# Two transformer blocks on one core: two bias tables stored another way, attention's softmax one head ahead, a norm in pairs of chunks

## The chip, the core and the metric

The kernel runs on 1 core of one Trainium2 chip. The metric is device time in microseconds (us) of one execution, lower is better. Engines are named as in the profile: PE is TensorE's matmuls, PEld its weight loads, DVE is VectorE, ACT ScalarE, POOL GpSimd, SP SyncE; ACTq and SPq are the DMA instructions that ACT and SP issue.

## The reference

Two blocks in a row over 256 tokens of width 2048, batch 1, all in float32. The parts that the change touches:

```python
# first block
mod = silu(c) @ w_ada + b_ada              # 2048 x 12288, split in six rows of 2048
shift_m, scale_m, gate_m, shift_f, scale_f, gate_f = split(mod, 6)
h = rms_norm(x, norm_mix_g) * (1 + scale_m) + shift_m
q, k, v, xs, z, bmat, cmat, dt = split(h @ w_in)
attn = rms_norm(moba_attention(q, k, v, rel_bias), attn_norm_g)  # 8 heads of 128; at 256
       # tokens plain causal: softmax(q k / sqrt(128) + rel_bias[rel_bucket(i - j)]) v
ssm = ssd_mixer(xs, z, bmat, cmat, dt, ...)    # conv of 4 taps, silu, state space, norm
x = x + gate_m * (concatenate([attn, ssm]) @ w_out)
h = rms_norm(x, norm_ffn_g) * (1 + scale_f) + shift_f
x = x + gate_f * conv_ffn(h, w_up, conv_w, conv_b, w_down)       # 2 x 5632 wide
x = rms_norm(x, final_norm_g)
# second block: neighbourhood attention on a 4 x 64 grid, its bias read from
# na_rpb (8 heads, 15, 31); latent attention; attention to a memory of 256 rows; swiglu
```

## The kernel before

**The weights** come as one stream of 442 tiles of 128 x 2048 float32 (1 MB), in the order of `STREAM`: xk, xv (keys and values of the memory, needed in the second block), xs, dt, bz, qkv, wb, wa, up, down, then the second block's. A tile is two halves; half h of the program is 24 matmuls of 256 columns (`half_T`) or 12 of 512 (`half_N`), because each product is made of three: high part by high part, low by high, high by low. So for each half ACT writes `w_hi` (`hi`, L474), POOL writes `w_lo` as the difference (L454), and PE multiplies (L1091 to L1095, L1105 to L1109). There are four slots for w_hi and w_lo and a ring of four raw tiles; SP issues tile t when POOL is done with the halves of tile t-4. The halves that matter here: xk from 0, xv from 32, xs from `hx` = 64, dt 80, bz from `hb` = 82, qkv from `hq` = 106, wb from 154, wa from `ha` = 170, up from `hu` = 186.

**The modulation rows.** silu(c) @ w_ada isn't made on PE: DVE adds up 192 rows of 128 x 1024 (0.5 MB each, `ada_row`, L1646, L1649), 32 for each sixth of `mod`. SP issues them between the tiles of the stream into a ring of four slots for the first 80 and of two slots behind that (`ADA_EARLY`). When they are used is set by the table `ROW_POINTS`, by straight lines between its points: `rows_by(h)` is the number of rows due at half h. SP issues by it (L401 to L411), and DVE calls `rows_to(h)` at many places between its other work. When 32 rows are in, ACT copies the sum (`slice_out`, L590, for the first three slices), PE sums over the partitions (`ada_sum`, 16 products with a column of ones, L1167), and DVE adds the bias (`ada_mod`). `ada_sum(4)` stands at PE ahead of half ha+12 and waits for all of the first 160 rows.

**The two tables.** Both attentions read their bias from DRAM with skewed access patterns. For the first, DVE leaves 8 rows of 512 in SBUF (`tab_row`), and ACT stores them 128 times each, one DMA of 1024 pieces of 2 KB into `rel_rows` (L612). For the neighbourhood one, 56 rows of 31 values are loaded into zeroed rows of 127 and stored 64 times each, 3584 pieces of 508 bytes into `rpb_rows` (L614). ACT issues both behind its tenth high part. ACT's DMAs run on queue q10, SP's on q1.

**Attention of the first block.** For each head u: PE `scores(u)`, DVE `front(u)` (bias and maximum, L1756, L1760), ACT `exp_head(u)` (L530), DVE `back(u)` (1/sum times the row, L1771, L1775), PE `turn(u)` (four transposes, L1345), ACT `copies(u)`, PE `values(u)` (L1358), ACT `moba_operand(u)` (L549, L551), DVE `moba_low(u)` (L1781). PE places two or three halves of qkv and wb in each turn of the loop (`beside`). DVE's turn u is `front(u+1)`, `back(u)`, `moba_low(u-1)`, `rows_to`.

**Output projection and feed-forward norm.** wa has four groups of four halves. After each, `wa_out(q)` scales the sum by the gate and the attention's row into SBUF (L2059), adds it to `res` (L2064) and signals; ACT squares that quarter of `res` (L494), DVE adds the squares up (L1701). ACT issues w_hi for the next halves behind its wait for that residual (L777 to L780). Ahead of `wa_out(q)` DVE brings its rows to ha+4q+4. After `wa_out(3)`: sum of squares over the partitions on PE (L1176), `means` and `root` on DVE (three Newton steps, L1676 to L1695), `token_scaled` (L1726), scale and shift on ACT (L787), `a_hi` (L505), `a_lo` (L1711), each in quarters of 4 chunks; then PE starts `up`.

## Time and profile before

| | |
|---|---|
| median of 3 runs | 3019.35 us (3014.46 to 3024.26) |
| profiled execution, its own time | 3018.35 us |
| its span | 3016.6 us |
| PE busy | 2789.4 us (92%) |
| PEld / POOL busy | 2711.5 us (90%) / 2197.0 us (73%) |
| DVE / ACT busy | 1072.8 us (36%) / 1210.7 us (40%) |
| mean granted TensorE clock | 0.955 of full speed |
| DMA | 589.75 MB, mean 196 GB/s |

The span is the stretch between the first and the last instruction in the trace; the execution's own time is 1.75 us longer. A busy PE is not PE at its peak: its matmuls overlap, so the time to look for is idle time ahead of a matmul, with what released it, and stretches where the granted clock is under 1.

### The profile page before, as it was taken

Reading aid. Unit: us, or ns where it says so; the run is one execution under the profiler, and the core shown is the slowest. Engines: PE = TensorE matmul, PEld = TensorE weight load, DVE = VectorE, ACT = ScalarE, POOL = GpSimd, SP = SyncE. Lnnn points to the kernel's source line nnn. Section 1 sums busy time; section 2 is a strip of 40 time slices with the busy share of each in tenths; the row PEclk is TensorE's granted clock in tenths of the full one; section 3 lists DMA queues with packets and bytes.
Section 4 is the critical chain, followed back from the end, with each engine's and each line's share of the span. In section 5 each row is a group of like instructions: output and inputs, shape, how many; then the busy total and the mean of one; then the engine's idle time right before and its main releaser. Section 6 shows DMA issues by size and latency. Waiting matters only on the chain.

```text
span 3016.6 us, 52183 instructions
## 1 busy us (share of the span) xinstructions
PE 2789.4 (92%) x21360; PEld 2711.5 (90%) x21360; DVE 1072.8 (36%) x1251; ACT 1210.7 (40%) x1439; POOL 2197.0 (73%) x889
## 2 busy tenths in 40 slices
PE   4799998977599999999999988999999999999997
PEld 3788998867599999999999977899999999999996
DVE  4554446646444544432235324461030000002233
ACT  3335343332253433334455344453353333334442
POOL 3577665545478889878888864586788888887894
PEclk7899899988799999999999999999999999999998
DMA  9897656555346666544545543363445555554552
GB/s 318 307 368 273 225 223 256 211 195 188 140 168 223 229 227 232 202 154 180 181 167 182 189 158 115 112 224 140 154 169 182 184 183 184 184 181 159 184 184 86
DMA packets 111618, 589.75 MB, mean 196 GB/s; under 512 B 23276, under 2 KB 25324, under 8 KB 54796
## 3 DMA queue, kind: packets, MB, share of 16 engines
q1 hardware_dynamic: 92592, 570.47, 52.0%
q10 hardware_dynamic: 18908, 17.58, 2.1%
q8 instruction: 90, 1.47, 0.2%
q14 instruction: 28, 0.23, 0.0%
HBM read 577.79 MB, written 10.21 MB: 195 GB/s over the span
## 4 chain that ended last, share of the span: by engine, by line
POOL 36%; issue 32%; PE 29%; DVE 1%; POOLq 1%; ACT 0%; DVEq 0%; ACTq 0%
POOL w_lo L454 36%; PE ps L1091 10%; PE ps L1095 10%; PE ps L1093 10%; POOLq L453 0%; PE ps L1176 0%; DVE res L2393 0%; POOLq L457 0%; ACT w_hi L474 0%; PE ps L1167 0%; DVE stage_v L1701 0%; DVE res L2064 0%; DVE ps L1685 0%; DVE ps L1682 0%; DVE rstd L1687 0%
## 5 line engine op out<-in xcount | busy, mean ns | idle before, releaser
L454 POOL TENSOR_TENSOR w_lo<-raw,w_hi 128x1024 fp32r<-128x1024 f32 x884 | 2196.6, 2499 | 785.8 <-ACT w_hi L474 783.0
L1091 PE MATMUL ps<-a_hi,w_hi 128*128 128x256 f32 x6512 | 1874.7, 288 | 117.2 <-POOL w_lo L454 43.5
L1093 PE MATMUL ps<-a_lo,w_hi 128*128 128x256 f32 x6512 | 1860.5, 286 | 0.0
L1095 PE MATMUL ps<-a_hi,w_lo 128*128 128x256 f32 x6512 | 1859.7, 286 | 0.0
L474 ACT CAST w_hi<-raw 128x1024 fp32r<-128x1024 f32 x884 | 918.3, 1047 | 1296.4 <-PE ps L1095 1135.4
L1091 PEld LDWEIGHTS ps<-a_hi,w_hi 128*128 128x128 f32 x6512 | 1270.2, 195 | 127.5 <-issue 52.7
L1093 PEld LDWEIGHTS ps<-a_lo,w_hi 128*128 128x128 f32 x6512 | 1269.7, 195 | 0.8
L1095 PEld LDWEIGHTS ps<-a_hi,w_lo 128*128 128x128 f32 x6512 | 1268.2, 195 | 0.0
L1808 DVE TENSOR_TENSOR a_lo<-arena,a_hi 128x1024 fp32r<-128x1024 f32 x44 | 107.6, 2448 | 348.4 <-ACT a_hi L816 348.4
L2356 DVE TENSOR_TENSOR work<-ps,rstd 128x512 f32<-128x512 f32 x22 | 15.2, 692 | 430.4 <-PE ps L1095 430.4
L1649 DVE SCALAR_TENSOR_TENSOR ps<-arena,small,ps 128x1024 f32<-128x1024 f32 x90 | 113.7, 1286 | 127.6 <-DMA arena<-ada 127.2
L1822 DVE TENSOR_SCALAR work<-ps,vec 128x256 f32<-128x256 f32 x100 | 47.5, 539 | 255.2 <-PE ps L1095 255.2
L1649 DVE SCALAR_TENSOR_TENSOR arena<-arena,small 128x1024 f32<-128x1024 f32 x60 | 111.3, 1865 | 74.0 <-DMA arena<-ada 73.6
L1105 PE MATMUL ps<-w_hi,a_hi 128*128 128x512 f32 x264 | 110.8, 420 | 5.0 <-POOL w_lo L454 5.0
L1107 PE MATMUL ps<-w_hi,a_lo 128*128 128x512 f32 x264 | 107.5, 407 | 0.0
L1109 PE MATMUL ps<-w_lo,a_hi 128*128 128x512 f32 x264 | 106.8, 404 | 0.0
L2119 DVE SCALAR_TENSOR_TENSOR arena<-arena,small 128x1024 f32<-128x1024 f32 x32 | 83.5, 2632 | 45.3 <-DMA arena<-ada 44.7
L1827 DVE SCALAR_TENSOR_TENSOR work<-ps,vec,work 128x255 f32<-128x255 f32 (+2 forms) x212 | 87.6, 476 | 5.5 <-DVE work L1822 2.4
L1105 PEld LDWEIGHTS ps<-w_hi,a_hi 128*128 128x128 f32 x264 | 52.6, 199 | 16.7 <-POOL w_lo L454 5.5
L1732 DVE TENSOR_TENSOR arena<-ps,rstd 128x1024 f32<-128x1024 f32 (+1 forms) x19 | 23.0, 1208 | 122.4 <-PE ps L1095 122.3
L1711 DVE TENSOR_TENSOR a_lo<-work,a_hi 128x1024 fp32r<-128x1024 f32 x24 | 46.2, 1926 | 50.8 <-ACT a_hi L505 50.8
L1109 PEld LDWEIGHTS ps<-w_lo,a_hi 128*128 128x128 f32 x264 | 52.4, 199 | 11.7
(181 smaller groups left out, 1266.5 us busy)
## 6 DMA issues: line engine op xcount, KB each, us to landing
raw<-stream SPq DMA_DIRECT2D x442, 1024.0 KB, 4.8
arena<-ada SPq DMA_DIRECT2D x192, 512.0 KB, 5.7
arena<-memT SPq DMA_DIRECT2D x4, 512.0 KB, 11.1
rel_rows<-arena ACTq DMA_DIRECT2D x1, 2048.0 KB
res<-xT SPq DMA_DIRECT2D x1, 2048.0 KB, 23.4
k_spill<-arena ACTq DMA_DIRECT2D x4, 512.0 KB, 8.7
v_spill<-arena ACTq DMA_DIRECT2D x4, 512.0 KB, 7.2
work<-rel_rows ACTq DMA_DIRECT2D x16, 128.0 KB, 2.2
```

The source lines that it names most:

```text
L454: pool.tensor_tensor(w_lo[:, h % SLOTS], raw_half(h), w_hi[:, h % SLOTS].bitcast(F32), ALU.subtract).then_inc(lo_ready, 1)
L474: act.copy(w_hi[:, base % 4], raw[:, tile_slot, (base % 2) * HALF:(base % 2 + 1) * HALF]).then_inc(hi_ready, 1)
L1091: pe.matmul(o, w_hi[:, h % SLOTS, w], a_hi[:, c0 + k, :], start=first and k == 0 and f % 2 == 0, stop=False, skip_group_check=True)
L1093: pe.matmul(o, w_hi[:, h % SLOTS, w], a_lo[:, c0 + k, :], start=False, stop=False, skip_group_check=True)
L1095: mm = pe.matmul(o, w_lo[:, h % SLOTS, w], a_hi[:, c0 + k, :], start=False, stop=last and k == 1, skip_group_check=True)
L1105: pe.matmul(out2[:, t, 0:width], a_hi[:, c0 + k, a], w_hi[:, h % SLOTS, w], start=first and k == 0, stop=False, skip_group_check=True)
L1107: pe.matmul(out2[:, t, 0:width], a_lo[:, c0 + k, a], w_hi[:, h % SLOTS, w], start=False, stop=False, skip_group_check=True)
L1109: mm = pe.matmul(out2[:, t, 0:width], a_hi[:, c0 + k, a], w_lo[:, h % SLOTS, w], start=False, stop=last and k == 1, skip_group_check=True)
L1649: ins = dve.scalar_tensor_tensor(out=a, in0=ada_slot(n % ring), scalar=ck, in1=a, op0=ALU.mult, op1=ALU.add)
L1808: dve.tensor_tensor(a_lo[:, a:a + 4, :], hidden[:, 4 * quad:4 * quad + 4, :], a_hi[:, a:a + 4, :].bitcast(F32), ALU.subtract).then_inc(hl_ ...
L1827: ins = dve.scalar_tensor_tensor(out=dst[:, c, shift:S], in0=src[:, c, 0:S - shift], scalar=w(c, taps - 1 - shift), in1=dst[:, c, shift:S] ...
L2119: dve.scalar_tensor_tensor(out=a, in0=ada_slot(s % 2), scalar=small[:, bass.ds(i * 2 + (16 + s // 2), 1)], in1=a, op0=ALU.mult, op1=ALU.ad ...
```

## The change

1. The neighbourhood table comes as an input in the layout in which it is read (56 x 64 x 127), so `rpb_rows`, its memset, its load and its store go.
2. `tab_row` moves to `stage_v`. Its store is cut into 8 DMAs, one head each (128 pieces of 2 KB from one partition), each behind two high parts of the halves 68 to 84.
3. xT is loaded in quarters behind tiles 5 to 8, not whole behind tile 6.
4. `ROW_POINTS` changes: 96 rows are due at half 97, not 104; between 148 and 182 the pace is 18 rows in 18 halves, then 14 in 16.
5. `slice_out(2)` moves up, ahead of the last four high parts of bz.
6. DVE's turn of the attention loop becomes `front(u+1)`, `back(u+1)`, rows, `moba_low(u-1)`.
7. `wa_out` works in PSUM; the rows stand behind it, and the last quarter is done in two halves.
8. The feed-forward norm: PE adds the last quarter's squares up itself, and scale, shift and split go in eight pairs of chunks, PE taking one pair per half.

```diff
-ROW_POINTS = [(-1, 8), (56, 64), (66, 64), (90, 84), (104, 96), (108, 96), (138, 128), (146, 128), (178, 160),
+ROW_POINTS = [(-1, 8), (56, 64), (66, 64), (97, 96), (108, 96), (138, 128), (148, 128), (166, 146), (182, 160),
               (186, 160)]
@@ sync
-                if t == 6:
-                    sp.dma_start(res[:, :, :], xT).then_inc(s_res, 16)
+                if 5 <= t < 9:
+                    q = t - 5
+                    sp.dma_start(res[:, 4 * q:4 * q + 4, :], xT[:, 4 * q:4 * q + 4, :]).then_inc(s_res[q], 16)
@@ scalar
-                if h == 6:
-                    act.wait_ge(rel_row, 1)
-                    act.dma_start(rel_dram, tab_row.unsqueeze(1).broadcast_to([8, P, REL])).then_inc(scr_stored, 16)
-                    act.wait_ge(rpb_in, 16)
-                    act.dma_start(rpb_dram, tab_rpb[:, 0:NA_W].unsqueeze(1).broadcast_to([56, GRID, NA_W]))\
-                       .then_inc(scr_stored, 16)
...
-            his(hx + 4, 8)
+            def rel_rows(h):
+                act.dma_start(rel_dram[h:h + 1], tab_row[h:h + 1].unsqueeze(1).broadcast_to([1, P, REL]))\
+                   .then_inc(scr_stored, 16)
+            for j in range(4):
+                his(hx + 4 + 2 * j, 2)
+                rel_rows(j)
...
-            his(hx + 13, 8)
+            for j in range(4):
+                his(hx + 13 + 2 * j, 2)
+                rel_rows(4 + j)
...
-                    his(hb + 19, 8)
-            slice_out(2)
+                    his(hb + 19, 4)
+                    slice_out(2)
+                    his(hb + 23, 4)
...
-            for q in range(4):
-                his(ha + 3 + 4 * q, 4 if q < 3 else 5)
+            his(ha + 3, 1)
+            for q in range(3):
+                his(ha + 4 + 4 * q, 4)
                 residual_ready("wa")(q)
                 square2(K0["ffn"] + q, res_quad(q))
+            his(ha + 16, 4)
@@ tensor
+            for n in range(8):
+                pe.wait_ge(fl_ready, n + 1)
+                half_of("T", "up", n)
+            groups("T", "up", 1, 22)
@@ vector
             front(0)
+            back(0)
             for u in range(8):
                 if u < 7:
                     front(u + 1)
-                back(u)
+                    back(u + 1)
...
+                rows_to(moba_until(2 * u))
...
-                rows_to(moba_until(2 * u + 1))
...
-            def wa_out(q):
+            def wa_out(q, a, b):
...
             for q in range(3):
-                rows_to(ha + 4 * q + 4)
-                wa_out(q)
+                wa_out(q, 0, 4).then_inc(evac[G % 2], 1)
                 if q:
                     add_up(K0["ffn"] + q - 1, early(q - 1))
+                rows_to(ha + 4 * q + 8)
...
+            def ffn_scaled(p):
+                for j in range(2):
+                    c = 2 * p + j
+                    ins = dve.scalar_tensor_tensor(out=ffn_pair(p)[:, j, :], in0=res[:, c, :], scalar=mod[:, 3, c:c + 1],
+                                                   in1=row_a, op0=ALU.mult, op1=ALU.mult)
+                ins.then_inc(fs_ready, 1)
```

In the order in which ACT issues its instructions, the place behind the last `v_spill` (the start of xs) read, before:

```order
L582 DMA v_spill<-arena 128x1024
L474 CAST w_hi<-raw 128x1024 x9
L663 ACTIVATE arena<-work 128x1024
L474 CAST w_hi<-raw 128x1024 x8
L663 ACTIVATE arena<-work 128x1024
```

and now (L482 is `hi`, L660 the store of one head, L670 the silu of a convolution):

```order
L588 DMA v_spill<-arena 128x1024
L482 CAST w_hi<-raw 128x1024 x2
L660 DMA rel_rows<-stage_v 128x1x512
...
L482 CAST w_hi<-raw 128x1024 x2
L660 DMA rel_rows<-stage_v 128x1x512
L482 CAST w_hi<-raw 128x1024
L670 ACTIVATE arena<-work 128x1024
```

Eight stores stand where none stood, four on each side of the first silu. On DVE, one turn of the attention loop (u = 5) read, before:

```order
L1756 SCALAR_TENSOR_TENSOR work<-ps,work 128x512
L1760 TENSOR_REDUCE small<-work 128x2
L1771 RECIPROCAL small<-small 128x2
L1775 TENSOR_SCALAR work<-work,small 128x256 x2
L1781 SCALAR_TENSOR_TENSOR a_lo<-ps,vec,a_hi 128x256
L1798 SCALAR_TENSOR_TENSOR res<-ps,mod,res 128x256 x4
L1649 SCALAR_TENSOR_TENSOR arena<-arena,small 128x1024 x3
```

and now (L1786 to L1811 are the lines L1756 to L1781 of before, L1679 a modulation row, L1828 the residual):

```order
L1786 SCALAR_TENSOR_TENSOR work<-ps,work 128x512
L1790 TENSOR_REDUCE small<-work 128x2
L1801 RECIPROCAL small<-small 128x2
L1805 TENSOR_SCALAR work<-work,small 128x256 x2
L1679 SCALAR_TENSOR_TENSOR arena<-arena,small 128x1024 x3
L1811 SCALAR_TENSOR_TENSOR a_lo<-ps,vec,a_hi 128x256
L1828 SCALAR_TENSOR_TENSOR res<-ps,mod,res 128x256 x4
```

The reciprocal now belongs to the head of the L1786 above it, and the rows stand ahead of the wait for the values. On DVE around the projection wa the rows (L1649, now L1679) and the residuals (L2059 and L2064, now L2091 and L2095) stood, before, as

```order
L1649 SCALAR_TENSOR_TENSOR arena<-arena,small 128x1024 x8
L2059 SCALAR_TENSOR_TENSOR work<-ps,mod,rstd 128x256 x4
L2064 TENSOR_TENSOR res<-res,work 128x1024
L1649 SCALAR_TENSOR_TENSOR arena<-arena,small 128x1024 x4
L2059 SCALAR_TENSOR_TENSOR work<-ps,mod,rstd 128x256 x4
```

and now

```order
L1679 SCALAR_TENSOR_TENSOR arena<-arena,small 128x1024 x5
L2091 SCALAR_TENSOR_TENSOR ps<-ps,mod,rstd 128x256 x4
L2095 TENSOR_TENSOR res<-ps,res 128x1024
L1679 SCALAR_TENSOR_TENSOR arena<-arena,small 128x1024 x7
L2091 SCALAR_TENSOR_TENSOR ps<-ps,mod,rstd 128x256 x4
L2095 TENSOR_TENSOR res<-ps,res 128x1024
L1731 TENSOR_REDUCE arena<-work 128x256
L1679 SCALAR_TENSOR_TENSOR arena<-arena,small 128x1024 x4
```

Five rows stand ahead of the first residual in place of eight, seven ahead of the second in place of four, and four ahead of the third in place of none.

## Rows read from the trace of the kernel before

**Rows 1.** The page: busy time, and the granted clock in 40 slices.

```profile
PE 2789.4 (92%) x21360; PEld 2711.5 (90%) x21360; DVE 1072.8 (36%) x1251; ACT 1210.7 (40%) x1439; POOL 2197.0 (73%) x889
PEclk7899899988799999999999999999999999999998
```

**Rows 2.** Timeline of PE, start: start us, us, instruction, idle before it, releaser.

```profile
80.48 0.55 PE L1091 MATMUL ps<-a_hi,w_hi 128*128 128x256 f32 x1 [33.44 <-issue]
112.36 0.58 PE L1091 MATMUL ps<-a_hi,w_hi 128*128 128x256 f32 x1 [12.53 <-POOL w_lo L454]
```

**Rows 3.** Timeline of ACT, the same stretch.

```profile
40.55 19.65 ACTq L614 DMA_DIRECT2D rpb_rows<-arena  x1
88.43 20.31 ACTq L582 DMA_DIRECT2D k_spill<-arena  x1
108.84 3.89 ACT L474 CAST w_hi<-raw 128x1024 fp32r<-128x1024 f32 x4 [19.38 <-issue]
```

**Rows 4.** Timeline of DVE, the same stretch.

```profile
73.60 1.29 DVE L1649 SCALAR_TENSOR_TENSOR ps<-arena,small,ps 128x1024 f32<-128x1024 f32 x1 [11.93 <-DMA arena<-ada]
79.90 0.42 DVE L1687 SCALAR_TENSOR_TENSOR rstd<-ps,rstd 128x256 f32<-128x256 f32 x1
```

**Rows 5.** DMA queues in 44 to 46 us, then in 47 to 54 us.

```profile
q10 hardware_dynamic: 103, 0.21, 33.5%
...
q10 hardware_dynamic: 174, 0.36, 45.8%
q1 hardware_dynamic: 90, 0.79, 37.3%
```

**Rows 6.** Windows: busy us by engine (PE, PEld, DVE, ACT, POOL), clock, DMA share, GB/s.

```profile
200.00:240.00 40.00, 40.00 (x178) 33.11 (x177) 17.95 (x14) 17.70 (x19) 35.28 (x16) 1.00 1.02 416
278.00:345.00 67.00, 66.37 (x480) 66.17 (x479) 31.62 (x50) 21.34 (x21) 47.17 (x21) 0.85 0.68 249
606.00:714.00 108.00, 77.88 (x447) 71.02 (x446) 43.95 (x64) 35.55 (x65) 48.39 (x20) 0.86 0.53 189
714.00:793.00 79.00, 54.68 (x398) 53.79 (x396) 47.86 (x50) 19.44 (x22) 39.96 (x17) 0.81 0.49 182
```

**Rows 7.** Timeline of PE and ACT at the third slice's sum.

```profile
422.29 6.99 PE L1167 MATMUL ps<-ones,arena 128*128 128x1 f32 x32 [6.52 <-ACT arena L590]
...
417.33 1.01 ACT L590 COPY arena<-ps 128x1024 f32<-128x1024 f32 x1 [6.25 <-DVE ps L1649]
```

**Rows 8.** Waits in 606 to 714 us: who for whom, total us, times, longest.

```profile
PE ps L1345 <- DVE work L1775: 30.1, 6, 7.2
ACT work L530 <- DVE small L1760: 37.8, 6, 9.4
...
DVE arena L1649 <- DMA arena<-ada: 8.4, 4, 2.6
```

**Rows 9.** Timeline of DVE, one bias of the attention loop, then projection wa.

```profile
685.80 0.69 DVE L1756 SCALAR_TENSOR_TENSOR work<-ps,work 128x512 f32<-128x512 f32 x1
...
759.47 1.28 DVE L1649 SCALAR_TENSOR_TENSOR arena<-arena,small 128x1024 f32<-128x1024 f32 x1 [2.43 <-DMA arena<-ada]
762.36 1.22 DVE L2064 TENSOR_TENSOR res<-res,work 128x1024 f32<-128x1024 f32 x1
```

**Rows 10.** Timeline of PE, projection wa: first stall, sum of the fifth slice.

```profile
768.09 0.58 PE L1091 MATMUL ps<-a_hi,w_hi 128*128 128x256 f32 x1 [14.12 <-POOL w_lo L454]
792.46 4.83 PE L1167 MATMUL ps<-ones,arena 128*128 128x1 f32 x32
```

**Rows 11.** Timeline of DVE, ACT and PE, feed-forward norm.

```profile
810.84 1.66 DVE L2059 SCALAR_TENSOR_TENSOR work<-ps,mod,rstd 128x256 f32<-128x256 f32 x4 [10.51 <-PE ps L1095]
827.88 2.36 DVE L1726 TENSOR_TENSOR work<-res,rstd 128x1024 f32<-128x1024 f32 x2
...
829.14 2.07 ACT L787 ACTIVATE work<-work,mod 128x256 f32<-128x256 f32 x4 [12.61 <-DVE work L1726]
...
833.69 0.55 PE L1091 MATMUL ps<-a_hi,w_hi 128*128 128x256 f32 x1 [11.42 <-DVE a_lo L1711]
```

More of the change, by code:

```diff
@@ L165, in rows_by, with block_program @@
             return n0 + (n1 - n0) * (h - a) // (b - a)
[L168 to L169 removed]
+def block_program(nc, stream, ada, xT, memT, vecs, consts, onehot, relb, rpb_dram, out, rel_dram,
+                  k_dram, v_dram):
     ctx = ExitStack()
@@ L269, in x_out, with ffn_pair @@
             return ps[:, 6:8, :].rearrange("p b (c t) -> p (b c) t", t=S)
+        def ffn_pair(p):
+            return work[:, 2048 + p % 4 * 512:2560 + p % 4 * 512].rearrange("p (c t) -> p c t", t=S)
         def early(k):
@@ L281, in stage @@
             return arena[:, 4096 + g % 2 * 1024:5120 + g % 2 * 1024]
-        s_const, s_vec, s_res = sem("s_const"), sem("s_vec"), sem("s_res")
+        s_const, s_vec = sem("s_const"), sem("s_vec")
+        s_res = [sem(f"s_res{q}") for q in range(4)]
         s_mem = [sem(f"s_mem{q}") for q in range(4)]
@@ L1388, in _ @@
             pe.wait_ge(row_ready, 2)
-            row_sums("ffn", (ps[:, 4, 0:S], early4))
-            groups("T", "up", 0, 22, al=al_before("ffn"))
+            pe.wait_ge(r_ready, NORM["ffn"])
+            for k in range(3):
+                pe.matmul(ps[:, 4, 0:S], ones[:, :], early(k), start=k == 0, stop=False, skip_group_check=True)
+            for p in range(2):
+                if p:
+                    pe.wait_ge(sq2_ready, K0["ffn"] + 4)
+                else:
+                    pe.wait_ge(last_sq, 1)
+                for j in range(2 * p, 2 * p + 2):
+                    mm = pe.matmul(ps[:, 4, 0:S], ones[:, :], sq2(K0["ffn"] + 3)[:, j, :], start=False, stop=j == 3,
+                                   skip_group_check=True)
+            mm.then_inc(r_summed, 1)
+            for n in range(8):
+                pe.wait_ge(fl_ready, n + 1)
+                half_of("T", "up", n)
+            groups("T", "up", 1, 22)
             ada_sum(5)
@@ L1841, in conv_ssm @@
                          lambda c: col("cs_b", 4 * j + c), 4, evac[G % 2])
-            dve.memset(tab_rpb, 0.0).then_inc(rpb_zero, 1)
             link(dve.memset(tab_row[:, S:REL], MASKED))
@@ L2051, in _ @@
             residual_part("wb", 3, 2)
[L2053 removed]
+            rows_to(ha)
+            def wa_out(q, a, b):
                 G = G0["wa"] + q
                 dve.wait_ge(half_used, ha + 4 * q + 4)
[L2057 to L2061 removed]
+                for j in range(a, b):
+                    o = acc(G)[:, j, :]
+                    ins = dve.scalar_tensor_tensor(out=o, in0=o, scalar=mod[:, 2, 4 * q + j:4 * q + j + 1],
+                                                   in1=row_b, op0=ALU.mult, op1=ALU.mult)
@@ L2070, in _ @@
                 if q:
                     add_up(K0["ffn"] + q - 1, early(q - 1))
-            rows_to(ha + 16)
+                rows_to(ha + 4 * q + 8)
+            add_up(K0["ffn"] + 2, early(2))
+            parts_ready(10)
             ada_mod(4)
-            add_up(K0["ffn"] + 2, early(2))
-            wa_out(3)
-            add_up(K0["ffn"] + 3, early(3))
-            parts_ready(11)
+            G = G0["wa"] + 3
+            wa_out(3, 0, 2).then_inc(last_res, 1)
+            link(wa_out(3, 2, 4))
@@ L2078, in _ @@
+            settle()
+            dve.engine_nop().then_inc(last_res, 1)
+            dve.engine_nop().then_inc(evac[G % 2], 1)
             v = ps[:, 4, 0:S]
             means("ffn", (v, D))
+            dve.engine_nop().then_inc(sq2_done, 1)
             root(v, ps[:, 4, S:2 * S], row_a)
-            token_scaled("ffn", 0, 5)
-            token_scaled("ffn", 1, 6)
-            for q in range(4):
-                low_of_ring("ffn", q, 4 * q)
-                if q < 2:
-                    token_scaled("ffn", q + 2, 7 + q)
+            def ffn_scaled(p):
+                for j in range(2):
+                    c = 2 * p + j
+                    ins = dve.scalar_tensor_tensor(out=ffn_pair(p)[:, j, :], in0=res[:, c, :], scalar=mod[:, 3, c:c + 1],
+                                                   in1=row_a, op0=ALU.mult, op1=ALU.mult)
+                ins.then_inc(fs_ready, 1)
@@ new lines, in ffn_low @@
+            def ffn_low(p):
+                dve.wait_ge(fh_ready, p + 1)
+                for j in range(2):
+                    c = 2 * p + j
+                    ins = dve.scalar_tensor_tensor(out=a_lo[:, c, :], in0=ffn_pair(p)[:, j, :], scalar=mod[:, 4, c:c + 1],
+                                                   in1=a_hi[:, c, :].bitcast(F32), op0=ALU.add, op1=ALU.subtract)
+                ins.then_inc(fl_ready, 1)
+            ffn_scaled(0)
+            ffn_scaled(1)
+            for p in range(8):
+                ffn_low(p)
+                if p < 6:
+                    if p >= 2:
+                        dve.wait_ge(fl_ready, p - 1)
+                    ffn_scaled(p + 2)
@@ L2509 @@
     scratch = [nc.dram_tensor(n, s, F32).ap() for n, s in
-               [("rel_rows", [8, P, REL]), ("rpb_rows", [56, GRID, NA_W]), ("k_spill", [4, P, 1024]),
+               [("rel_rows", [8, P, REL]), ("k_spill", [4, P, 1024]),
                 ("v_spill", [4, P, 1024])]]
```

50 lines of the change are left out of this document (23 added, 27 removed).

## The prediction

> **What bounds the kernel now.** I read the page first: PE is busy 92% of the span and its clock is full except in the first third and a few slices behind it [rows 1]. So the time to win is where PE stands idle, and the slow matmuls behind each such stop; the rest of the span is one half of weights after the other, 2.88 us each. I then went through PE's timeline for idle time over 0.8 us. Its largest stops lie at places that this change touches: the start, the third slice's sum, the attention loop, the projection wa, the feed-forward norm. Each place is read from the timelines of the engines PE waits for. Sums are made against the profiled execution's 3018.35 us, 1.0 under the median of 3019.35; I add that 1.0 at the end.
>
> **1. Start: the tables' stores go, -34.** PE stands 33.4 us until 80.5 and 12.5 us until 112.4 [rows 2]. ACT's issue of the 3584 pieces took 19.65 us, and the next issue on its queue, a `k_spill`, 20.31 us, behind the same backlog; ACT converted nothing meanwhile [rows 3]. The first stop ends with DVE's root, which waited for modulation rows: the fourteenth was used at 73.6 and the root ended at 80.3 [rows 4]. What made the row late is on the queues: in 47 to 54 us q10 held 46% of the DMA engines' time and the stream got 0.79 MB in 7 us, 113 GB/s [rows 5], where 416 is had with q10 quiet [rows 6]. Without the stores, row 13 has ahead of it tile 6, a quarter or two of xT and row 12, some 2.5 MB behind 44 us, at 0.41 MB/us 6 us, with some 2 us of latency by 52 to 54; row 13 and the root take 7 [rows 4], so PE starts at about 60: 20 us won. The second stop goes wholly, 12.5. Each stop is followed by matmuls at 0.5 of the clock; one fewer is worth 2 us. Sum 34. Against it, the DMA has less time for the same rows: 25 MB are due between 43 us and the first slice's end, 62 us of transfer where PE leaves 68. So at worst 14 of the 34 come back; at best 37.
>
> **2. The first table head by head, +42.** The 8 stores now fall in 278 to 345 us. The trace has one such store: 8 partitions at once. In its first 2 us it moved 0.21 MB in 103 pieces at 33.5% of 16 engines' time, so 0.10 us of one engine per piece; then, steady, 0.36 MB in 7 us, 51 GB/s from 8 partitions, and by the same sum 0.29 us per piece [rows 5]. A head is 0.26 MB from one partition, on however many engines. Its ends: 16 engines at 0.10 us per piece, 0.8 us; or one partition giving an eighth of 51 GB/s, 41 us. At first a piece of 2 KB, which lies in one partition, took 0.10 us, 20 GB/s, so the slow end is far off; at 20 GB/s a head takes 13 us, at 51 GB/s 5. I take 9, 72 us in all. Meanwhile the stream gets little, as in 47 to 54 us. The stretch has 32% of its DMA time idle, 21 us [rows 6], and the four halves that stand converted ahead of PE cover 11. Three more modulation rows than before (4 us) fall in it too. 72 + 4 - 21 - 11 = 44; rounded to 42, as the dt products, slow and without weights, lie in it. Between the ends the cost is 0 to 270. ACT's own issues (0.4 us each) hide under its 68% idle time.
>
> The profile shows 8 partitions giving 51 GB/s between them when the store runs steadily [rows 5]. The Trainium skill (SBUF — State Buffer, Door 1: The DMA port swizzle) says that DMA bandwidth depends on how many of the 16 ports the partitions reach, four neighbouring partitions sharing one at about 27 GB/s. By that rule the 8 partitions are two ports, and the trace agrees (51); a single partition is one port, an estimate of 9.7 us per head, and this term would be 48 in place of 42.
>
> **3. Third slice's sum, -9.** PE waits 6.5 us for ACT's copy, which waits for DVE's last rows of the slice, and the sum then runs 7.0 us at the low clock [rows 7], where the later one takes 4.8 [rows 10]. With the 96th row due seven halves sooner and the copy ahead of four high parts, wait and slow clock go: 6.5 + 2.2. Not late: at up to 3.7 us per row, 2.4 of wait and 1.3 of work [rows 9], the nine rows behind bz's first convolution (which ends at 368) end near 400 us, and PE needs them at 415.
>
> **4. Attention loop, -30.** `turn(u)` waits for DVE's L1775 six times, 30.1 us [rows 8]. Cause: DVE does `front(u+1)` and `back(u)` only after two or three rows and the wait for the values of head u-1. Now the probabilities for turn u+1 are ready a whole turn early. New waits: `back(u+1)` follows ACT's `exp_head(u+1)`, 1.4 us, within the same turn, and DVE stands through it. A turn of DVE is then some 1.4 (front, two instructions of 0.7 [rows 9]) + 1.5 + 0.8 (back) + 6 (three rows, two of them landed, one at 2.4 + 1.3 [rows 9]) + 0.5, 10.2 us, against PE's 11.2 (three halves and 2.6 of attention); in the first four turns 2 rows and 2 halves stand against each other likewise. ACT waits 37.8 us for the maximum [rows 8]; that shrinks, so the high parts come sooner. The clock over this stretch is 0.86 [rows 6]; with 30 us of stops gone I take 3 us back from it, and give 3 to small new waits.
>
> **5. Projection wa, -13.** The stretch 714 to 793 us has 54.7 us of PE work in 79 [rows 6]. Its largest stop, 14.1 us [rows 10], is ACT waiting for the first residual, which ended at 763.6 behind eight rows [rows 9]. Now five rows stand there, and the first residual is done some 31 us behind the last head's values at 714 (heads' sum 5, root and two residuals 10, rows 13, residual 3), in time. But the others stand behind it. Once DVE waits for each, the ring of two slots gives a row per 3.7 us [rows 9]; beside less POOL work I take 3.3. Seven rows, two of them landed, are 19 us and put the second residual at 53; the last four are in at 64, and `ada_sum(4)` waits for them. PE, with sixteen halves, would be there at 47, and so waits 17 us; before it was there at 792.5 - 714 = 78 [rows 10]. Gain 15, less 2 for a slow clock behind the new stop.
>
> **6. Feed-forward norm, -9.** From the last half of wa to the first matmul of `up`: 810.8 to 833.7, 22.9 us [rows 11]. Its terms now: half a residual 1.7 (2 of the 4 of 1.66, and an add), then square, second half and its products to 5.2, means and root 5.5 (as 74.8 to 80.3 [rows 4]), one pair scaled 0.9, ACT 1.1 (half of 2.07), low part 0.9: 14. Later pairs come every 2 us and a half takes 2.9, so PE doesn't wait again. The ninth high part ACT can only give at about 25 us, needed at 28: just hidden.
>
> Sum: -34 + 42 - 9 - 30 - 13 - 9 = -53; 3018.35 - 53 + 1.0 = **2966 us**. The memset, load and store of the second table cost nothing more, and the second block is untouched.
>
> **The rivals.**
> - *A head's store is quick* (2 us or less). For: 0.10 us per piece at first [rows 5]; 16 engines share it. Against: the steady rate. Then term 2 is 0 to 5: 2926.
> - *The store of one partition starves the stream: slower.* Place: 278 to 360 us. With a head at h us the cost is 8h - 28; it cancels the 95 us won elsewhere at h = 15. For: 51 GB/s over 8 partitions could be a limit of each partition or a clash of 16 engines on one. Against: one engine alone drew 20 GB/s. At h = 20: 132, so 3018 - 95 + 132 = 3055.
> - *The rows' ring sets the pace from 610 to 790.* If the 32 rows of the fifth slice can't go faster than the 3.7 us of [rows 9] when tiles and DVE's other work come between, `ada_sum(4)` moves by 13 of the 43 us of terms 4 and 5 only: 2996. Against: DVE waited only 8.4 us for rows in the loop [rows 8].
> - *The start stays bound by DMA*: the rows land as late as now since xT and tiles fill the queue; only the second stop goes, 22 us less won: 2988.
>
> **How the numbers follow.** Forecast 0.49 (own range 2945 to 2990), quick store 0.20, starved stream 0.12, ring 0.12, start 0.07. A measurement here tells about 0.3%, 9 us, from no change: faster below 3010, slower above 3028. The range goes from the quick store's value with some 10 us of room, 2916, to 3008, above the ring's and the start's; outside lie the starved stream and a tail of the forecast. Faster 0.86 (all but the starved stream, and a little of the others' tails), slower 0.09, same 0.05.
>
> **What would show it.** Right: no ACTq issue near 20 us; PE starts before 65 us and has no second stop by 90. In 280 to 370 us q10 at 25 to 30 GB/s and PE stops of 40 us in all, with DVE waiting for rows. No L1805 wait at PE ahead of 700 us. A wait of some 15 us at the fifth `ada_sum` for DVE's rows. Norm 14 us. Wrong: a head's 128 pieces taking under 3 us or over 13; stops in the loop of over 10 us in all; the second residual ahead of PE's need.

## The result, and the profile after

| | before | changed |
|---|---|---|
| median, us | 3016.9 (3011.1 to 3024.3, 4 runs) | **2964.7** (2962.4 to 2966.8, 4 runs) |
| profiled span, us | 3016.6 | 2960.6 |

The ratio is 0.9824, with a 95% interval from 0.9808 to 0.9839: 52 us less, where 53 less was predicted. The sum is right, but not all of its terms are: terms 2 and 3 together came out 15 us better than forecast and term 5 came out 13 us worse. That they cancel is luck. The spans differ by 56.0 us.

The page of the changed kernel, engines and granted clock [rows 1]:

```profile
PE 2771.9 (94%) x21366; PEld 2694.1 (91%) x21366; DVE 1106.1 (37%) x1274; ACT 1205.9 (41%) x1436; POOL 2211.4 (75%) x889
PEclk8998799998899999999999999999999999999998
```

PE has nearly the same count of matmuls in both, and 17.5 us less of modelled busy time. That is fewer of them at the low clock; the rest of the 56 us is idle time. To place it I set landmarks of PE side by side: the first matmul of a slice's sum (its weights are `ones`, 32 of them in a row), the last product of the last head, and the first matmul of `up`.

```
landmark                          before    after    gained since the one above
first slice's sum                 153.17   119.79    33.4   (term 1: 34)
fourth slice's sum                587.25   571.65   -17.8   (terms 2 and 3: -33)
last head's last product          714.7    666.9     32.2   (term 4: 30)
fifth slice's sum                 792.46   744.27     0.4   (term 5: 13)
first matmul of up                833.69   778.30     7.2   (term 6: 9)
end of the span                  3016.6   2960.6      0.6
```

Everything arises ahead of `up`. The landmark of the fourth sum is good to some 6 us: in four kernels that have the same instructions up to there (the changed one, and those below with the old loop, the old last rows and the old norm) it starts between 571.7 and 578.0 us. PE's timeline of the changed kernel has, in the order of the program, these stops [rows 2, 10, 11]:

```profile
60.80 0.55 PE L1107 MATMUL ps<-a_hi,w_hi 128*128 128x256 f32 x1 [14.37 <-issue]
...
287.29 0.58 PE L1107 MATMUL ps<-a_hi,w_hi 128*128 128x256 f32 x1 [15.56 <-POOL w_lo L462]
...
672.59 0.58 PE L1107 MATMUL ps<-a_hi,w_hi 128*128 128x256 f32 x1 [5.27 <-DVE res L1828]
...
744.27 6.96 PE L1183 MATMUL ps<-ones,arena 128*128 128x1 f32 x32 [18.49 <-issue]
...
778.30 0.58 PE L1107 MATMUL ps<-a_hi,w_hi 128*128 128x256 f32 x1 [8.40 <-DVE a_lo L2130]
```

The first stop ends at 60.8, where about 60 was expected, and there is no second one until the stores of the table. The last but one is the wait that the new order makes, 18.5 us at the fifth sum. Windows of the changed kernel, to be read against [rows 6]: the table's stores, the attention loop, projection wa, the norm. (Columns as there: busy us of PE, PEld, DVE, ACT and POOL, clock, DMA share, GB/s.)

```profile
245.00:325.00 80.00, 53.48 (x383) 52.98 (x381) 25.69 (x42) 14.26 (x14) 37.22 (x16) 0.75 1.00 175
590.00:667.00 77.00, 71.02 (x453) 65.34 (x451) 61.43 (x60) 38.30 (x73) 56.08 (x20) 0.96 0.66 231
667.00:744.00 77.00, 49.95 (x388) 48.59 (x386) 63.75 (x56) 19.91 (x22) 50.69 (x18) 0.85 0.58 216
744.00:778.00 34.00, 24.04 (x142) 22.66 (x142) 17.31 (x33) 8.08 (x11) 11.93 (x5) 0.75 0.37 140
```

In the first, the DMA engines are busy all the time and move 175 GB/s. PE lacks weights for a third of the stretch, and ACT and POOL, which prepare them, are idle too. In the second, the clock is 0.96 where it was 0.86, and PE is busy 92% of the time. The waits of that stretch (who for whom, total us, times, longest) have no line for the probabilities any more [rows 8]; the new ones are small:

```profile
DVE small L1801 <- ACT work L538: 8.1, 7, 1.2
...
PE ps L1361 <- DVE a_lo L1811: 4.6, 2, 3.0
```

In the third window, DVE is busy 63.8 us of 77, the largest share that it has anywhere in the table.

### The profile page after: what moved, and what is told of

It is laid out like the page before. It is cut to its first block, busy times and chain, and to the rows that moved or that the text cites. A ratio compares the mean times of both kernels' runs of the same rounds, so it can differ in the third digit from the quotient of the medians.

```text
span 2960.6 us, 52233 instructions
## 1 busy us (share of the span) xinstructions
PE 2771.9 (94%) x21366; PEld 2694.1 (91%) x21366; DVE 1106.1 (37%) x1274; ACT 1205.9 (41%) x1436; POOL 2211.4 (75%) x889
## 4 chain that ended last, share of the span: by engine, by line
POOL 37%; issue 31%; PE 30%; DVE 1%; POOLq 1%; ACT 0%; DVEq 0%; ACTq 0%
POOL w_lo L462 37%; PE ps L1107 10%; PE ps L1109 10%; PE ps L1111 10%; POOLq L461 0%; PE ps L1183 0%; POOLq L465 0%; DVE res L2448 0%; PE ps L1192 0%; DVE stage_v L1731 0%; ACT w_hi L482 0%; DVE ps L1715 0%; DVE ps L1712 0%; DVE rstd L1717 0%; DVE ps L2091 0%
## 5 line engine op out<-in xcount | busy, mean ns | idle before, releaser
L482 ACT CAST w_hi<-raw 128x1024 fp32r<-128x1024 f32 x884 | 918.4, 1047 | 1262.1 <-PE ps L1111 1124.3
L1679 DVE SCALAR_TENSOR_TENSOR ps<-arena,small,ps 128x1024 f32<-128x1024 f32 x90 | 114.1, 1286 | 141.2 <-DMA arena<-ada 140.9
L1679 DVE SCALAR_TENSOR_TENSOR arena<-arena,small 128x1024 f32<-128x1024 f32 x60 | 142.8, 2397 | 50.4 <-DMA arena<-ada 50.2
L2174 DVE SCALAR_TENSOR_TENSOR arena<-arena,small 128x1024 f32<-128x1024 f32 x32 | 84.8, 2670 | 44.0 <-DMA arena<-ada 43.5
L1123 PEld LDWEIGHTS ps<-w_hi,a_lo 128*128 128x128 f32 x264 | 52.2, 198 | 10.5
```

The source lines that it names most:

```text
L482: act.copy(w_hi[:, base % 4], raw[:, tile_slot, (base % 2) * HALF:(base % 2 + 1) * HALF]).then_inc(hi_ready, 1)
L1123: pe.matmul(out2[:, t, 0:width], a_lo[:, c0 + k, a], w_hi[:, h % SLOTS, w], start=False, stop=False, skip_group_check=True)
L1679: ins = dve.scalar_tensor_tensor(out=a, in0=ada_slot(n % ring), scalar=ck, in1=a, op0=ALU.mult, op1=ALU.add)
L2174: dve.scalar_tensor_tensor(out=a, in0=ada_slot(s % 2), scalar=small[:, bass.ds(i * 2 + (16 + s // 2), 1)], in1=a, op0=ALU.mult, op1=ALU.ad ...
```

## The experiments

The first question was the table: what do the eight stores cost, and what makes them slow? The landmarks give terms 2 and 3 only together. (Pieces and rows taken one by one, here and below, are from the trace's records; medians are of 2 to 5 runs.)

**Stores taken from all 128 partitions.**

```diff
-tab_row = stage_v[0:8, 0:REL]
+tab_row = stage_v[:, 0:REL]
+tab_wide = arena[0:32, 6656:6784]
...
-pe.matmul(ps[0:8, 1, 0:S], tab_rel, tab_hot[:, 0:S],
+pe.matmul(ps[:, 1, 0:S], tab_wide, tab_hot[:, 0:S],
...
+dve.tensor_copy(tab_wide.rearrange("p (h r) -> p h r", r=16), tab_rel.unsqueeze(2).broadcast_to([32, 8, 16]))
...
-act.dma_start(rel_dram[h:h + 1], tab_row[h:h + 1].unsqueeze(1).broadcast_to([1, P, REL]))
+act.dma_start(rel_dram.rearrange("h (q r) n -> (h q) r n", r=8)[:, h], tab_row)
```

> The changed kernel (2964.7 us), with each row of the first table made sixteen times (128 partitions instead of 8) and each of the eight stores taken from all 128 partitions, 128 pieces of 2 KB as before and at the same places of the program. In the changed kernel a head's store takes 7.1 to 10.4 us and its pieces 0.81 us each in the mean. Theory A, the reading side is what is slow (one partition gives some 28 GB/s): pieces fall to 0.10 to 0.16 us, a store to 1 to 2 us, and nearly all of the 30.6 us that PE loses between the first half of xs and the first of qkv comes back: 2935 to 2943 us. Theory B, many small writes of 2 KB are slow whatever they are read from: 2965 us, a store still 7 to 10 us.

Measured: 2934.8 us, ratio to before 0.9721 (0.9705 to 0.9737).

**Stores from four neighbouring partitions**, from the same widened table:

```diff
-act.dma_start(rel_dram[h:h + 1], tab_row[h:h + 1].unsqueeze(1).broadcast_to([1, P, REL]))
+act.dma_start(rel_dram[h].rearrange("(q r) n -> q r n", r=32),
+              tab_row[16 * h:16 * h + 4].unsqueeze(1).broadcast_to([4, 32, REL]))
```

> The changed kernel (2964.7 us), with head h stored from four neighbouring partitions (16h to 16h+3), 32 pieces of 2 KB from each, at the same places. Theory A1, four neighbouring partitions share one way out: a store takes 8 to 10 us as from one partition, 2965 us. Theory A2, each partition has its own limit of some 28 GB/s: 2.5 us per store, 2938 to 2946 us. Theory B (the writes are slow): 2965 us as well, and only the run with 128 partitions tells it from A1. The Trainium skill (SBUF - State Buffer, Door 1) is on the side of A1: four neighbouring partitions share one port of about 27 GB/s; by it a store of 0.26 MB is an estimate of 9.7 us here too.

Measured: 2951.5 us, ratio 0.9772 (0.9755 to 0.9788), between the two theories.

**No stores.**

```diff
-                rel_rows(j)
...
-                rel_rows(4 + j)
...
-            act.wait_ge(scr_stored, 16 * NH)
...
+            "rel": np.broadcast_to(np.pad(a["rel_bias"][onehot[:, :S].argmax(0)].T[:, None, :], ((0, 0), (0, 0), (0, REL - S)),
+                                          constant_values=MASKED), (8, P, REL))
```

> The changed kernel without the eight stores of the first table: its rows come as an input, gathered when the inputs are laid out. It prices the whole of the stores. If they alone cost the 30.6 us between the first half of xs and the first of qkv: 2932 to 2937 us, with PE's stops near 287, 325 and 369 us gone. Rival: modulation rows and the dt products hold PE there anyway: 2950 to 2960 us.

Measured: 2933.2 us, ratio 0.9718 (0.9701 to 0.9734). So the stores cost 31.5 us, and from 128 partitions, where a store takes 2.2 us in the mean, next to nothing (1.6 us, within the intervals). The DMA queues in 240 to 330 us: the changed kernel, where ACT's queue is q10 (with it 272 pieces of other stores) and SP's is q1:

```profile
q10 hardware_dynamic: 1296, 2.62, 59.3%
q1 hardware_dynamic: 2786, 14.55, 39.2%
```

The same with stores from four partitions:

```profile
q1 hardware_dynamic: 4020, 20.49, 66.4%
q10 hardware_dynamic: 1200, 2.62, 11.2%
```

And from 128:

```profile
q1 hardware_dynamic: 4878, 24.62, 72.2%
q10 hardware_dynamic: 1296, 2.62, 8.1%
```

The windows of the same kernels over the 84 us of the stores, changed kernel first, then four partitions, then 128:

```profile
244.00:328.00 84.00, 56.82 (x397) 56.32 (x398) 28.55 (x48) 17.01 (x17) 39.01 (x18) 0.74 0.99 182
```

```profile
244.00:328.00 84.00, 74.15 (x532) 73.45 (x531) 34.93 (x52) 22.79 (x23) 52.28 (x23) 0.84 0.78 258
```

```profile
244.00:328.00 84.00, 83.36 (x622) 83.16 (x621) 42.66 (x62) 26.71 (x26) 61.17 (x26) 0.88 0.81 311
```

The bytes on q10 are the same in all three. From one partition they hold 59% of the engines' time, from 128 they hold 8%, and q1 moves 24.6 MB in place of 14.6. One 2 KB piece takes 0.81 us in the mean from one partition and 0.09 from 128. The run with four partitions separates two things. Its stores are no quicker: eight of them one behind the other from 245.2 to 323.0 us, 2.1 MB at 27 GB/s, and a head's store in the changed kernel takes 7.1 to 10.4 us from its first piece to its last, 8.6 in the mean, 31 GB/s. So four neighbours give together no more than one gives, and A2 falls. Yet the stream gets 20.5 MB beside these stores, which hold 11% of the engines' time. **With the same bytes in about the same time, the store that holds more of the engines' time costs the others more**: 31.5 us with the long pieces, 18 with the short ones. The 18 us come with the engines' time nearly free of the stores, so the share isn't all of it. The tiles of the stream still land late beside the four partitions (issues in 240 to 330 us, the last number is the median time to landing; changed kernel, four partitions, 128):

```profile
raw<-stream SPq DMA_DIRECT2D x10, 1024.0 KB, 18.8
```

```profile
raw<-stream SPq DMA_DIRECT2D x12, 1024.0 KB, 17.6
```

```profile
raw<-stream SPq DMA_DIRECT2D x14, 1024.0 KB, 6.6
```

What holds them is not shown.

The Trainium skill (SBUF — State Buffer, Door 1: The DMA port swizzle) gives about 27 GB/s to four neighbouring partitions that share a port, and the run with four partitions agrees, 27 GB/s. A second page (DMA: Bandwidth & Descriptors, Why a DMA increments its semaphore by 16 and not by 1) says that the slowest dimension longer than one sets how many engines a DMA is spread over: by it 16 for the 128 rows, four for the 4 x 32. Fewer engines would fit the smaller share of 11%, but no record here names the engine of a piece, so it isn't shown.

**One of the two tables out of the start.** In the kernel before, the neighbourhood table comes as in the change and the first one is stored at its old place:

```diff
-                    act.wait_ge(rpb_in, 16)
-                    act.dma_start(rpb_dram, tab_rpb[:, 0:NA_W].unsqueeze(1).broadcast_to([56, GRID, NA_W]))\
-                       .then_inc(scr_stored, 16)
```

> The kernel before (3019.2 us), with only the second table (the neighbourhood one) given ready for use; the first one is stored at its old place, all heads at once from 8 partitions. It parts the 34 us of the start between the two stores. Theory A, the first store alone (2 MB from 8 partitions, at 51 GB/s some 41 us from 44 us on) is what delays the rows: PE's stops stay above 25 us in all and the time is 3005 to 3019 us. Theory B, the second store, of 1.8 MB, is what holds them, since its 56 partitions make 2560 of the 3584 pieces: the stops shrink to 12 us as in the changed kernel, 2985 to 2990 us.

Measured: 3002.8 us, ratio 0.9953 (0.9934 to 0.9972). PE's timeline has one large stop left:

```profile
79.00 0.55 PE L1086 MATMUL ps<-a_hi,w_hi 128*128 128x256 f32 x1 [32.57 <-issue]
```

Neither theory had it whole. (The second store alone is 3584 pieces; the 2560 of the expectation is a slip.) With the first store, 1024 pieces from 43.5 to 87.5 us (48 GB/s from 8 partitions), the first stop [rows 2] stays; without the second store the second one is gone, and both stores have to leave the start: the first sum starts at 137.4 us here, 15.7 sooner than before, and 17.6 sooner still in the changed kernel. That last step also has the load of xT in quarters, which no run takes by itself.

**The third slice as before.**

```diff
-ROW_POINTS = [(-1, 8), (56, 64), (66, 64), (97, 96), (108, 96), ...
+ROW_POINTS = [(-1, 8), (56, 64), (66, 64), (90, 84), (104, 96), (108, 96), ...
...
-                    his(hb + 19, 4)
-                    slice_out(2)
-                    his(hb + 23, 4)
+                    his(hb + 19, 8)
+            slice_out(2)
```

> The changed kernel (2964.7 us), with the copy of the third slice behind eight high parts and its rows due where they were before. By the step of the prediction: 9 us back, 2973 us, with a stop of about 6.5 us at the third sum. Rival: the table's stores have PE behind there, the rows come in time whatever their due points, and only the copy's place counts: 0 to 3 us, 2965 to 2968 us.

Measured: 2963.6 us, ratio 0.9827 (0.9801 to 0.9852), no difference. The stop is back:

```profile
410.23 6.99 PE L1182 MATMUL ps<-ones,arena 128*128 128x1 f32 x32 [6.08 <-ACT arena L596]
```

But PE got to the first half of qkv 7 us sooner (391.0 against 398.2 by POOL's subtraction for it), since three rows fewer had to come between the stores. The move wins its stop and pays for it where the DMA is short. In the run without stores nothing is paid: from the second slice's sum to the third's it takes 163.7 us, before 176.2, 12.4 less.

**The loop in its old order.**

```diff
             front(0)
-            back(0)
             for u in range(8):
                 if u < 7:
                     front(u + 1)
-                    back(u + 1)
+                back(u)
...
-                rows_to(moba_until(2 * u))
...
+                rows_to(moba_until(2 * u + 1))
```

> The changed kernel with the attention loop in its old order (front of the next head, then back of this one, rows behind it). Up to the last head's values the changed kernel won 32 us by the new order. Theory A, the terms add: 2964.7 + 32 = 2997 us. Theory B, the rows' ring of two slots sets when the fifth sum can start: PE stands 18.5 us there in the changed kernel, and a loop that ends later gives the rows time, so only 32 - 18 = 14 us come back, 2979 us, with the stop at the fifth sum under 5 us.

Measured: 2990.8 us, ratio 0.9904 (0.9887 to 0.992), 26 back. The six stops for L1805 (before: L1775) return:

```profile
PE ps L1361 <- DVE work L1805: 29.3, 6, 7.2
```

By the landmarks 34 us are lost at the last head's values and 28 at the fifth sum. But 6.4 of them are already lost at the fourth sum, ahead of the loop, where both kernels have the same instructions; from there to the last head's values it is 27.7. The stop at the fifth sum stays at 18.2. So the terms add, nearly, and theory B is wrong: the rows don't run ahead when the loop is slower.

**The last rows as before.**

```diff
-(148, 128), (166, 146), (182, 160)
+(146, 128), (178, 160)
...
             for q in range(3):
+                rows_to(ha + 4 * q + 4)
                 wa_out(q, 0, 4).then_inc(evac[G % 2], 1)
-                rows_to(ha + 4 * q + 8)
```

> The changed kernel (2964.7 us), with the last rows of the fifth slice placed as before (eight rows ahead of the first residual of wa, then four ahead of each, the rows due in even steps). By the step of the prediction that gave the new order 13 us, 2978 us, with a stop of PE near 14 us at the first residual. The trace of the changed kernel says otherwise: from the last head's values to the fifth sum it takes 77.0 us, and took 77.4 before. By that the order is worth nothing, 2963 to 2968 us: what is won at the first residual is stood at the fifth sum.

Measured: 2959.5 us, ratio 0.9813 (0.9788 to 0.9838). The 13 us of term 5 don't exist. The stop only changes its place: 19.6 us at 731.1, as the kernel before had 14.1 there [rows 10], in place of 18.5 at the sum:

```profile
731.12 0.55 PE L1107 MATMUL ps<-a_hi,w_hi 128*128 128x256 f32 x1 [19.58 <-POOL w_lo L462]
```

With two runs, its 5 us below the changed kernel are within both intervals. In the traces the sum itself takes 3.6 us here and 7.0 where it stands right behind the stop.

**Four landing slots for the fifth slice's rows**, on top of the 128 partitions:

```diff
-                ring = 4 if n < ADA_EARLY else 2
+                ring = 2 if ADA_EARLY <= n < 128 else 4
...
+            if i >= 4:
+                return arena[:, 6144 + 1024 * (i - 4):6144 + 1024 * (i - 3)]
```

> The run with the table stored from 128 partitions (2934.8 us), with four landing slots in place of two for the 32 modulation rows of the fifth slice (the two more lie where the convolved x of the state-space part was, free by then). PE stands 18.2 us at the fifth sum for DVE's last row, and of the 55.8 us that DVE takes there for 16 rows, three residuals and their like, only 29 are work. Theory A, the ring of two slots sets the pace of the rows: the stop goes or shrinks to under 5 us, 2914 to 2922 us. Theory B, DVE's own work and the order of its steps set it (DVE is 83% busy between 665 and 744 us in the changed kernel): the stop stays above 12 us, 2929 to 2935 us.

Measured: 2925.1 us, ratio 0.9696 (0.9675 to 0.9716). The stop at the fifth sum is 14.9 us:

```profile
707.49 4.82 PE L1190 MATMUL ps<-ones,arena 128*128 128x1 f32 x22 [14.90 <-issue]
```

Both theories are half right, and the groups of DVE and POOL in 655 to 710 us say why (count, then busy us and mean ns of one, then idle before):

```profile
L1691 DVE SCALAR_TENSOR_TENSOR arena<-arena,small 128x1024 f32<-128x1024 f32 x16 | 42.5, 2718 | 0.0
```

```profile
L469 POOL TENSOR_TENSOR w_lo<-raw,w_hi 128x1024 fp32r<-128x1024 f32 x14 | 43.0, 3086 | 13.2 <-ACT w_hi L489 13.2
```

DVE waits for no transfer now (0.0), and still a row takes 2.72 us, where the rows of [rows 9] took 1.28. Taken one by one, a row beside none of POOL's subtractions takes 1.28, the ones wholly beside one 3.40. So the next run gives these rows a second operand in PSUM. It leaves out that they add to the fifth slice's sum (the expectation calls that vector the sixth), so it prices the wait and is no kernel to use:

```diff
-ins = dve.scalar_tensor_tensor(out=a, in0=slot, scalar=ck, in1=a,
+b = ps[:, 5, S:2 * S].unsqueeze(1).broadcast_to([P, 4, S]) if alone[0] and s == 4 else a
+ins = dve.scalar_tensor_tensor(out=a, in0=slot, scalar=ck, in1=b,
```

> The run with four landing slots (2925.1 us), with the last 16 or so modulation rows of the fifth slice, behind the last head, reading a row of PSUM in place of the accumulator in SBUF as their second operand. What is left out: those rows' accumulation, so the sixth modulation vector is another. In the run with four slots DVE waits for no transfer there, and yet PE stands 14.9 us at the fifth sum: 8 of 16 rows lie wholly beside a subtraction of POOL and take 3.40 us in the mean, those beside none 1.28, and the subtraction 3.28 instead of 2.41. Theory A, two instructions with two operands in SBUF, one on DVE and one on POOL, run one after the other: with one operand in PSUM all rows take 1.2 to 1.4 us, POOL's 2.4, the stop at the fifth sum goes, 2906 to 2913 us. Theory B, the rows are slow for another reason (the landing transfers write beside them, the accumulator's address): durations and stop stay, 2923 to 2927 us. The Trainium skill (SBUF - State Buffer, Who interferes with whom) is on the side of A: a DVE instruction with two SBUF inputs contends with a GpSimd instruction that reads SBUF.

Measured: 2908.4 us, ratio 0.9634 (0.961 to 0.9657). The same two groups, in 652 to 692 us:

```profile
L1695 DVE SCALAR_TENSOR_TENSOR arena<-arena,small,ps 128x1024 f32<-128x1024 f32 x16 | 19.6, 1274 | 5.3 <-DMA arena<-ada 5.3
```

```profile
L469 POOL TENSOR_TENSOR w_lo<-raw,w_hi 128x1024 fp32r<-128x1024 f32 x13 | 31.1, 2406 | 11.9 <-ACT w_hi L489 11.9
```

2718 ns to 1274 and 3086 to 2406, by the place of one operand; the stop at the fifth sum falls from 14.9 to 3.5 us:

```profile
691.09 6.18 PE L1190 MATMUL ps<-ones,arena 128*128 128x1 f32 x32 [3.53 <-issue]
```

This is the rule of the Trainium skill (SBUF — State Buffer, Who interferes with whom): a DVE instruction with two SBUF inputs contends with a GpSimd instruction that reads SBUF, and one waits until the other is through. The numbers of the run with four slots agree: the longest rows take 3.42 us, 2.14 more than alone, and the subtraction beside such a row ends some 2.3 us after the row's start, 1.1 us before the row's end.

**Two placings on that base.** First the four slots with the last rows as in the kernel before (the edit shown above):

> The run with four landing slots (2925.1 us), with the last rows placed as in the kernel before (fewer in the loop, eight ahead of the first residual of wa). On the changed kernel this placing gave 2959.5 in place of 2964.7 us. If DVE's rows beside POOL's subtractions are what is short there, wherever they stand: 2919 to 2926 us. If four slots and the late rows stand against each other (more rows in one piece wait for their transfers): 2927 to 2932 us.

Measured: 2914.9 us, ratio 0.9658 (0.9641 to 0.9676), the lowest median of all runs that leave nothing out, and 50 us below the changed kernel. Not all of the 10 us that it gains is the placing's: in its trace 6.6 us are won ahead of the fourth sum (537.1 against 543.8 us), where both kernels have the same instructions. That the placing is worth some 4 us, as on the changed kernel, stays unproved. Then with the sum carried on in PSUM:

```diff
+if alone and s == 4:
+    first = part_ not in alone
+    alone.add(part_)
+    b = a if first else ada_part(part_)
+    a = a if n >= 158 else ada_part(part_)
```

> The fastest run so far (2914.9 us: table from 128 partitions, four landing slots, last rows placed as before), with the fifth slice's sum carried on in PSUM from the last head on: of its last 14 rows the first even and the first odd one read the accumulator in SBUF, the others have one operand there, and the last two write the whole sum back to SBUF, so that nothing is left out. If rows beside POOL's subtractions are what holds the last product of wa (PE stands 10.7 us there), they fall from 3.4 to 1.3 us, and so much of the stop goes as the rows waiting for their transfers leave: 2903 to 2909 us. If four slots can't bring rows faster than DVE takes them now, 2911 to 2915 us.

Measured: 2915.4 us, ratio 0.9665 (0.9646 to 0.9684), no gain, as the expectation's second case has it. Its rows are fast:

```profile
L1697 DVE SCALAR_TENSOR_TENSOR ps<-arena,small,ps 128x1024 f32<-128x1024 f32 x10 | 12.6, 1282 | 7.1 <-DMA arena<-ada 7.1
L1697 DVE SCALAR_TENSOR_TENSOR ps<-arena,small 128x1024 f32<-128x1024 f32 x2 | 6.4, 3260 | 0.0
L1697 DVE SCALAR_TENSOR_TENSOR arena<-arena,small,ps 128x1024 f32<-128x1024 f32 x2 | 2.6, 1276 | 2.3 <-DMA arena<-ada 2.3
```

The second line is the two rows that still read both operands from SBUF, 3.26 us each beside 1.28. But DVE now waits 9.4 us for transfers. The queue in 660 to 688 us:

```profile
q1 hardware_dynamic: 2160, 10.49, 93.4%
```

That is 375 GB/s from engines that are nearly always busy, right behind 10 us (646 to 656) in which the DMA moved next to nothing, 2 GB/s. SP stood there for a slot that DVE had to free (waits of SP in 640 to 662 us):

```profile
SPq L393 <- DVE ps L1697: 19.6, 1, 19.6
```

So the next bound looks to be the transfer, which starts too late. No run tests that.

**The norm as before.**

```diff
-            for p in range(8):
-                act.wait_ge(fs_ready, p + 1)
...
+            for q in range(4):
+                k = tmp_before("ffn") + q
+                act.wait_ge(xr_ready, 5 + q)
...
-            wa_out(3, 0, 2).then_inc(last_res, 1)
-            link(wa_out(3, 2, 4))
+            wa_out(3, 0, 4).then_inc(evac[G % 2], 1)
```

> The changed kernel (2964.7 us) with the feed-forward norm as before: the fourth residual whole, and scale, high and low part by four chunks. By the marks of the two traces the change is worth 7.2 us from the fifth sum to the first matmul of up, by the prediction 9: 2971 to 2974 us, with PE standing about 7.9 and 11.4 us where it now stands 1.2 and 8.4 us. Rival: the wait at the fifth sum, which stands just ahead, hides the last residual, and only the first pair's work counts: 2966 to 2969 us.

Measured: 2974.4 us, ratio 0.9852 (0.983 to 0.9874), 9.7 more than the changed kernel. By its own trace 7.7 of them lie between the fifth sum and `up`; the rest lies ahead, where the instructions are the same. PE stands 6.2 and 11.4 us, as before.

## Why the prediction was right, and where not

1. **Start, -34.** 33.4 by the landmark, PE at 60.8 where 60 was worked out. Right in size. The run with one table shows that the two stores share it; how much of it is the xT quarters', no run shows.
2. **First table head by head, +42.** Measured 31.5, by the run without stores. A head took 8.6 us where 9 was taken; but 9 was a choice between 5 and 13, so that it came so near is in part luck. That the reading side is the limit, which the prediction had only among its reasons, is shown by the 128 partitions. What was mis-sized is "the stream gets little": during the 68.6 us in which stores ran, it got 7.0 MB, 17 us' worth at 416 GB/s. 68.6 + 4 - 17 - 21 - 11 is 24; I put the rest of the 31.5 down to the low clock, 0.75 in this stretch, which no run separates. (The upper end of the cost, 270, is a slip: at 41 us a head the prediction's own 8h - 28 gives 300.)
3. **Third slice's sum, -9.** The stop and the slow clock went, as said, and the stretch wins 12.4 us where the DMA is free. Beside the stores three more rows take back 7, which are part of the 31.5 of term 2. I had 4 for them there. Terms 2 and 3 together are -17.8 in the table above, in place of -33.
4. **Attention loop, -30.** 32.2 by the landmarks, 26 by the run with the old order (27.7 in the loop of its trace). The stops for the probabilities are gone, and the new waits are small, 1.2 us of DVE for ACT's exponentials seven times. Right.
5. **Projection wa, -13.** Wrong; it gave 0.4. The step that failed is "the first residual is done some 31 us behind the last head's values". It took 40.8. DVE's timeline around that head (its low part is L1811, the heads' sum L1818):

```profile
661.16 6.51 DVE L1679 SCALAR_TENSOR_TENSOR arena<-arena,small 128x1024 f32<-128x1024 f32 x2 [2.10 <-DMA arena<-ada]
669.40 1.56 DVE L1679 SCALAR_TENSOR_TENSOR arena<-arena,small 128x1024 f32<-128x1024 f32 x1 [1.72 <-DMA arena<-ada]
670.89 1.65 DVE L1828 SCALAR_TENSOR_TENSOR res<-ps,mod,res 128x256 f32<-128x256 f32 x4
672.46 0.86 DVE L1811 SCALAR_TENSOR_TENSOR a_lo<-ps,vec,a_hi 128x256 fp32r<-128x256 f32 x2
673.24 3.72 DVE L1818 TENSOR_REDUCE arena<-arena 128x256 f32<-128x2048 f32 x1
```

   PE's last product for the head ends at 667.3, but three rows and a residual stand ahead of the low part: 6 us that were not in my count, and PE stood 5.3 us behind them. The five rows that I put at 13 took 16.9. From there on I was right (23 us to the second residual for 22, 13 to the last row for 11), and the wait at the fifth sum is 18.5 for 17, but everything was 10 to 13 us late. Behind it stands a wrong reading of [rows 9]: I took the 1.28 us of two rows that stood beside no subtraction for the price of a row. In the changed kernel's stretch 18 rows and 18 subtractions at 1.28 and 2.41 us are 66 us of 77, one after the other, so by this sum no order of the rows could have won much, and the run with the old order shows no gain from the new one.

```profile
L462 POOL TENSOR_TENSOR w_lo<-raw,w_hi 128x1024 fp32r<-128x1024 f32 x18 | 53.4, 2984 | 26.3 <-ACT w_hi L482 26.3
L1679 DVE SCALAR_TENSOR_TENSOR arena<-arena,small 128x1024 f32<-128x1024 f32 x18 | 45.1, 2525 | 10.1 <-DMA arena<-ada 10.1
```

   These are the groups of 667 to 744 us. In the page the same kernel's 90 rows that add to PSUM take 1286 ns in the mean and the 60 that add in SBUF 2397. The page of before has 1286 and 1865 for the same two groups: the split was there to be read.
6. **Feed-forward norm, -9.** 7.2 by the landmark, 9.7 by the run with the old one, of which 7.7 lie in the norm's own stretch. Right.

Of the rivals, the quick store and the starved stream fell with the 8.6 us per head; the start did not stay bound by the DMA. The third one, that the rows set the pace of the fifth slice, is what happened to term 5, if not through the two slots alone: two more slots gave 9.7 us, one operand in PSUM another 16.7. Those 16.7 are a price and not a gain that was had: the run that keeps the whole sum (2915.4 us) stood for its transfers instead.

## What to carry to other kernels

Store a small table from as many partitions as can be had: widening it cost one copy and a wider matmul here and gave 30 us, and a store that must be slow should at least hold little of the DMA engines' time (18 us of cost in place of 31.5). Before pricing a DVE instruction with two operands in SBUF, look at what POOL does beside it, and group its rows by where the second operand lies; the mean of each group is its price as long as POOL is as busy there. When a sum of terms comes out right, set landmarks and compare it term by term, since two errors of 13 and 15 us left no trace in the total.

## What was not expected of the hardware

- One partition gave 31 GB/s to a store and four neighbouring ones together 27, but the pieces of the first were 0.81 us long on the DMA engines and those of the second 0.13.
- A DVE row of 128 x 1024 took 1.28 us alone, 3.40 beside a POOL subtraction, and 1.28 beside it with one operand in PSUM; the subtraction took 2.41 us alone and 3.14 in the mean (up to 3.39) beside rows with both operands in SBUF.
- Stores of 2.1 MB in all, read from one partition at a time, left all queues together 182 GB/s over 84 us; read from 128 partitions, the same stores left 311.
